# Seven half-size products in place of eight for three input projections, and a transform moved behind them

## The chip, the cores and the metric

One core of one Trainium2 chip runs the whole program. The metric is the device time of one execution in microseconds (us); lower is better.

The engines: TensorE (PE in the profile; its weight loads are PEld), the Vector engine (DVE), the Scalar engine (ACT), GpSimd (POOL), and the Sync engine (SP), which only issues DMAs. All matrix work is float32; the profile records each float32 matmul as two passes, so counts of matmul records are twice those of the code.

## What is computed

One layer of a diffusion backbone on 640 tokens (128 context, 512 latent) of width 1024: modulated norm, a token mixer (an mLSTM part and a Hyena part side by side), norm, and a mixture of 16 experts. The change touches the Hyena part alone:

```python
proj = xm @ p['w_in']                  # xm: 640 tokens x 1024
hy_in = proj[..., ML_QKVO_COLS + ML_GATE_COLS:]       # 3 x 512 columns
u = short_conv(hy_in, p['hy_conv_w'], grid)           # 3 taps along the tokens, per channel
parts = jnp.split(u, HY_ORDER + 1, axis=-1)           # three inputs of 512 channels
z = parts[-1]
for n in range(HY_ORDER):
    z = parts[n] * long_conv(z, filt[n, 0], filt[n, 1], p['hy_bias'][n])   # by FFT
```

## The kernel before

Everything lives in one SBUF tensor (`arena`) and one PSUM tensor of 8 banks (`banks`, 512 float32 columns each). Each engine runs one hand-written program in order; the order of work is set by these programs and by named semaphores. A semaphore counts finished steps (`conv_d` 3 means three short convolutions done).

**Weights** arrive as 21 chunks of 2 MB in a ring of three slots (`chunks`, from line 346), issued by SP at L410 once the chunk three places before has been consumed (`freed`). Chunks 0 to 9, 12 and 14 are pieces of `w_ada` (the modulation), 10, 11 and 13 (`HY_AT`) the three Hyena inputs in the order part 2, part 0, part 1, and 15 to 18 the mLSTM's q, k, v, o.

**Ahead of the Hyena part**, TensorE makes the filters' spectra, then turns the normed input `x_raw` (ten times four transposes, L1716); ACT (L734, L738) and DVE (L1069, L1073) apply the modulation on the way out of PSUM and so write `hT`, the transposed activations, 8 blocks of 128 rows by 640 tokens. Then come `ada_piece(8)` and `ada_piece(9)` (L1622).

**The projections** (`hyena_group(n)`, n = 0 to 11): one group makes 128 channels of one input. `channel_groups` (L1721 to 1727) runs over the 8 row blocks k and multiplies the same 128 x 128 weights with the 512 latent columns (L1725) and the 128 context columns (L1726) of `hT`, into two banks. ACT (`taps`, L752, L753) reads both banks and multiplies by the middle tap; DVE (`short_conv`, L1087 to L1090) adds the outer taps, again from the banks. The first eight results are turned to tokens in rows (`to_tokens`, L1736, L1737) and copied out by ACT (`untranspose`, L759, L760); the last four stay as they are in `part1t`.

**The order**: groups 0 to 8, each followed by the transposes of the one before, with `ada_turn` and `ada_piece` 10 and 11 in between; `ada_turn(2)`; the first forward transform `forward(0)` (L1757, L1759, ten bank fills, copied out by ACT in `spectra`, L778); groups 9 to 11; `project_qk(0)`, four groups of the same form; a transpose of the packed modulation vectors (L1798) and the first inverse transform (L1804, L1808, L1809); `forward(1)`; `project_qk(1)`; and so on.

Beside this, DVE runs after `forward(0)`: `spectrum_of(0)`, `short_conv(9)`, `low_products(0)`, `short_conv(10)`, `high_products(0)`, `short_conv(11)`, `high_sums`, a butterfly (which signals `mul_done` 1), `context_products(0)` (`mul_done` 2), then `ada_columns(1)`, `ada_columns(2)` and four small operations that end in `modB_ready`. TensorE waits for that last signal ahead of L1798:

```python
        project_qk(0)
        pe.wait_ge(S["ld_dft"], 48)
        pe.wait_ge(S["modB_ready"], 1)
        pe.transpose(ps[0:64, 0, 0:P], pack...)          # L1798
        for t in range(NT):                              # first inverse transform
```

Of the kernel before, what the change touches and what calls it, by code (L numbers as in the profile page):

```python
# [13 lines left out]
P = 128  # L14
# [13 lines left out]
ORD = 2  # L28
# [77 lines left out]
def emit(nc, a, stack):  # L106
# [116 lines left out]
    ada_rows = [area(W1 + 6144, CH), area(W4, CH), area(W4 + CH, CH)]  # L223
# [55 lines left out]
    def rt(*shape):  # L279
# [25 lines left out]
    names = """ld_setup ld_mlp ld_w3 ld_hybias ld_dft ld_x ld_late ld_gate ld_state ld_rowctx ld_rowlat  # L305
        ld_x2 ld_route ld_gr2 rows_stored y_zeroed out_stored  all_stored
        ada_done ada_row ada_t mod_ready setup_t cols_ready cvec_ready mlp_done arg_ready hid_ready ones_ready x_rstd xn_ready
        win_ready filt_done filt_read spec_read sq_ready sq_done lanes_read norm_done norm_sqrt norm_stored norm_cols xrs_ready comb_done ab_ready modA_ready modB_ready
        xt_done xt_a xt_d hy_done taps_ready conv_a conv_d tp_done tp_read fw_done fe_read mul_done iv_done iv_read
        packT_ready qk_done qk_read kt_done gate_done gate_read gt_done gt_read row_a row_ready m_ready  # L310
# [3 lines left out]
        lg_done rt_v rt_exp pos_done idx_done tiles_ready route_ready  # L314
# [25 lines left out]
    freed.update({n: ("hy_done", NB * (i + 1)) for i, n in enumerate(HY_AT)})  # L340
# [51 lines left out]
    def _(sp):  # L392
# [70 lines left out]
        sp.wait_ge(S["out_stored"], 64 + 16 * SPILL)  # L463
# [23 lines left out]
    def _(pool):  # L487
# [33 lines left out]
        pool.wait_ge(S["filt_read"], 28)  # L521
        pool.dma_start(area(W6, 1536), a["late"]).then_inc(S["ld_late"], 16)
# [5 lines left out]
                       zeros.unsqueeze(1).broadcast_to((P, KD * KD, P))).then_inc(S["y_zeroed"], 16)  # L528
# [31 lines left out]
        pool.wait_ge(S["out_stored"], 64)  # L560
        pool.wait_ge(S["y_zeroed"], 16)
# [60 lines left out]
    def _(act):  # L622
# [119 lines left out]
        def taps(n):  # L742
            part, blk = ((2, 0, 1)[n // 4], n % 4)
            act.wait_ge(S["hy_done"], n + 1)
            if part != 2:
                act.wait_ge(S["taps_ready"], 2)
            if n >= 2:
                act.wait_ge(S["tp_done"], min(n - 1, 8))
            u = part1t[:, blk, :] if part == 1 else ubuf[:, n % 2, :]
            w = tap(part, blk, 1)  # L750
            b = 1 + 2 * (n % 2)
            link(A(u[:, CTX:TOK], ps[:, b, :], ACT.Copy, scale=w[0]))  # L752
            link(A(u[:, 0:CTX], ps[:, b + 1, 0:CTX], ACT.Copy, scale=w[1]), "conv_a")  # L753

        def untranspose(n):
            blk = n % 4
# [5 lines left out]
        for n in range(9):  # L762
            taps(n)
            if n == 8:
                ada_row(2)
            if n:
                untranspose(n - 1)
# [22 lines left out]
        for n in range(9, 12):  # L790
# [1357 lines left out]
```

## Time and profile before

| | |
|---|---|
| median of 3 runs | 829.66 us (828.74 to 830.28) |
| the profiled execution's own time | 835.36 us |
| its span, first to last instruction | 833.5 us |
| mean granted TensorE clock | 0.985 |
| PE busy | 788.0 us (95% of the span) |
| DVE, ACT, POOL busy | 417.9, 278.2, 111.0 us |
| PE busy on L1725 and L1726 | 164.2 and 61.5 us, 320 records each |
| PE share of the chain that ended last | 84% |

Times in the rows below are from the start of the span. A busy time of a matmul holds its way through the array, which overlaps with the next one; the pace of a stream of matmuls is read from the starts.

### The profile page before, as it was taken

To read this page: it belongs to the slowest core of one execution; us is meant where nothing else is said; L and a number is where in the kernel's file an instruction comes from. 1 tells how busy PE (TensorE), PEld (TensorE's weight loads), DVE (VectorE), ACT (ScalarE), POOL (GpSimd) and SP (SyncE) were. 2 spreads that over 40 slices of the span, in tenths; PEclk is the share of its full clock that TensorE was granted. 3 is DMA by queue.
4 is the path that set the end of the run, shared out by engine and by line. 5 is a ranking of instruction groups with operands and counts; after the bars stand their busy time and mean duration, and the time that the engine had idled before them with its cause. 6 is when DMAs were issued, how large, how long until landed. Compare 5 with 4: busy or idle time off the path is not lost.

```text
span 833.5 us, 16962 instructions
## 1 busy us (share of the span) xinstructions
PE 788.0 (95%) x6753; PEld 457.1 (55%) x6753; DVE 417.9 (50%) x763; ACT 278.2 (33%) x558; POOL 111.0 (13%) x217
## 2 busy tenths in 40 slices
PE   4999899999999999999999999689999999999975
PEld 1232455554555457456775445357777777777741
DVE  3567622223891496664547475833333333333327
ACT  1567802224110211246233243223333333333325
POOL 4000100000001000011002000032222222222221
PEclk9999999999999999989999999889999999999999
DMA  8987450213051802133008574989999999999537
GB/s 257 390 345 298 169 202 3 99 48 155 0 202 57 250 1 102 26 128 114 13 2 314 198 282 150 410 351 423 419 417 416 418 419 420 416 418 416 217 109 289
DMA packets 41973, 195.11 MB, mean 234 GB/s; under 512 B 4873, under 2 KB 5237, under 8 KB 34301
## 3 DMA queue, kind: packets, MB, share of 16 engines
q1 hardware_dynamic: 29944, 156.70, 47.4%
q0 software_dynamic: 9216, 31.10, 10.7%
q10 hardware_dynamic: 2758, 6.52, 2.2%
q8 instruction: 42, 0.69, 0.3%
q14 instruction: 13, 0.11, 0.0%
HBM read 175.75 MB, written 18.55 MB: 233 GB/s over the span
## 4 chain that ended last, share of the span: by engine, by line
PE 84%; DVE 6%; DMA 3%; ACT 3%; issue 3%; POOL 1%; ACTq 0%; DVEq 0%; POOLq 0%
PE banks L2079 20%; PE banks L1725 17%; PE banks L2092 10%; PE banks L1863 4%; PE banks L1726 4%; PE banks L1872 4%; PE banks L1967 3%; PE banks L1670 2%; PE banks L1957 2%; DMA arena<-in_x_sample 2%; PE banks L1622 2%; PE banks L1757 2%; PE banks L1692 1%; PE banks L1925 1%; PE banks L1917 1%
## 5 line engine op out<-in xcount | busy, mean ns | idle before, releaser
L2079 PE MATMUL banks<-arena 128*32 128x256 f32 x3072 | 176.4, 380 | 1.1 <-DVE arena L1548 1.1
L1725 PE MATMUL banks<-arena 128*128 128x512 f32 x320 | 164.2, 595 | 1.5 <-issue 0.8
L2079 PEld LDWEIGHTS banks<-arena 128*32 128x32 f32 x3072 | 120.5, 110 | 48.6 <-issue 2.1
L1726 PEld LDWEIGHTS banks<-arena 128*128 128x128 f32 x320 | 60.8, 190 | 76.5 <-issue 76.5
L2092 PE MATMUL banks<-arena 128*32 128x256 f32 x1536 | 93.0, 379 | 1.2 <-DVE arena L1552 1.2
L1528 DVE STREAM_TRANSPOSE arena<-arena 128x256 f32<-128x256 f32 x49 | 32.1, 655 | 122.5 <-PE banks L2079 113.9
L2092 PEld LDWEIGHTS banks<-arena 128*32 128x32 f32 x1536 | 60.1, 110 | 24.2 <-DVE arena L1552 1.7
L1726 PE MATMUL banks<-arena 128*128 128x128 f32 x320 | 61.5, 274 | 0.0
L928 ACT ACTIVATE arena<-banks 32x256 f32<-32x256 f32 x98 | 36.8, 375 | 71.3 <-PE banks L2092 70.7
L1535 DVE COPY arena<-banks 32x256 f32<-32x256 f32 x98 | 41.4, 422 | 33.0 <-PE banks L2092 32.3
L1725 PEld LDWEIGHTS banks<-arena 128*128 128x128 f32 x320 | 48.6, 192 | 4.8 <-issue 3.3
L590 POOL DMA_INDIRECT arena<-expert_input,arena x47 | 46.4, 987 | 12.4 <-issue 12.4
L1087 DVE SCALAR_TENSOR_TENSOR arena<-banks,arena 128x504 f32<-128x504 f32 x12 | 8.9, 743 | 70.0 <-ACT arena L753 70.0
L752 ACT ACTIVATE arena<-banks,arena 128x512 f32<-128x512 f32 x12 | 8.2, 687 | 97.9 <-PE banks L1726 97.9
L944 ACT ACT_TABLE_LOAD x24 | 30.8, 1283 | 28.7 <-issue 17.1
L947 ACT ACTIVATE arena<-banks 128x128 f32<-128x128 f32 x48 | 13.4, 279 | 79.5 <-PE banks L2079 79.5
L1863 PE MATMUL banks<-arena 128*128 128x512 f32 x80 | 37.6, 632 | 0.0
L1872 PE MATMUL banks<-arena 128*128 128x512 f32 x80 | 36.1, 594 | 0.0
L1967 PE MATMUL banks<-arena 128*128 128x512 f32 x80 | 35.2, 595 | 0.0
L1957 PE MATMUL banks<-arena 128*128 128x512 f32 x80 | 35.2, 593 | 0.0
L587 POOL COPY arena<-arena 128x1 int32 x47 | 8.6, 183 | 163.6 <-DVE arena L1528 163.6
L1863 PEld LDWEIGHTS banks<-arena 128*128 128x128 f32 x80 | 16.1, 204 | 20.1 <-issue 20.1
(388 smaller groups left out, 995.9 us busy)
## 6 DMA issues: line engine op xcount, KB each, us to landing
arena<-in_w_gate SPq DMA_DIRECT2D x15, 2048.0 KB
arena<-in_w_down SPq DMA_DIRECT2D x15, 2048.0 KB
arena<-in_w_up SPq DMA_DIRECT2D x14, 2048.0 KB
arena<-in_w_ada SPq DMA_DIRECT2D x12, 2048.0 KB, 10.1
arena<-in_w_in SPq DMA_DIRECT2D x7, 2048.0 KB, 8.0
expert_output<-arena ACTq DMA_DIRECT2D x49, 128.0 KB
expert_output<-arena POOLq DMA_DIRECT2D x1, 4096.0 KB, 20.4
arena<-in_w_out SPq DMA_DIRECT2D x2, 2048.0 KB, 8.0
```

Source lines behind the costliest of these rows:

```text
L590: pool.indirect_dma_start(xr[n], None, h2_quarters, bass.IndirectOffsetOnAxis(ap=idx_now[n], axis=0))\
L928: ins = act.activation(ysb[n][:, l * 256:(l + 1) * 256], ps[l * LANE:(l + 1) * LANE, 5, 0:256], ACT.Copy)
L1528: dve.transpose(xg, xr[n].rearrange("p (r k) -> p k r", k=KD)).then_inc(S["xg_ready"], 1)
L1535: ins = dve.tensor_copy(ysb[n][:, l * 256:(l + 1) * 256], ps[l * LANE:(l + 1) * LANE, 5, 0:256])
L1725: M(ps[:, b, :], lhs, hT[:, k, CTX:TOK], start=k == 0, stop=k == KD - 1)
L1726: mm = M(ps[:, b + 1, 0:CTX], lhs, hT[:, k, 0:CTX], start=k == 0, stop=k == KD - 1)
L1863: mm = M(ps[:, 1 + n % 4, :], hT[:, k, n * P:(n + 1) * P], w[:, k, :], start=k == 0, stop=k == KD - 1)
L1872: mm = M(ps[:, 1, :], hT[:, k, t * P:(t + 1) * P], w[:, k, :], start=k == 0, stop=k == KD - 1)
L1957: M(ps[:, 1 + 2 * (j % 2) + c, :], part1t[:, k, t * P:(t + 1) * P], w[:, NB + k, :], start=k == 0, stop=False)
L1967: mm = M(ps[:, 1 + 2 * (j % 2) + c, :], ymlT[:, k, t * P:(t + 1) * P], w[:, k, :], start=False, stop=k == NB - 1)
L2079: mm = M(ps[q * LANE:(q + 1) * LANE, 2, 0:2 * P].rearrange("p (g a j) -> p g a j", g=2, j=LANE), xg[:, k, :], gate_up[e % 3][:, :, k, q, : ...
L2092: mm = M(ps[l * LANE:(l + 1) * LANE, 5, 0:256], aT[:, q * LANE:(q + 1) * LANE], w[:, q, l * 256:(l + 1) * 256], start=q == 0, stop=q == FF ...
```

## The change

For each pair of 128-channel blocks the product (1024 rows by 256 channels) x (1024 rows by 640 tokens) is cut in two along the rows, the channels and the tokens. In place of eight half-size products it does seven (Winograd's form of Strassen's scheme), from sums of quarters of the weights (`wsums`) and of the activations (`hs1` to `hs4`), and adds the seven results into two buffers of 640 tokens (`raw`) in SBUF. Each product is 4 matmuls of 128 x 128 weights on 320 columns. DVE makes the sums and all but the first of the additions; ACT copies the first product. `taps` and `short_conv` now read `raw` and not the banks. The blocks are taken in the order 0, 2, 1, 3 of each input.

All twelve blocks (six pairs) now come ahead of `forward(0)`, whose spectral work on DVE and ACT is no longer interleaved with three groups. `ada_piece(8)` moves ahead of the wait for the filters (before the transposes of L1716), `ada_piece(9)` between the first two products. `cosine_halves(1)` and the gate columns move into the pair loop on DVE. The load of `late` on POOL's queue waits for all convolutions rather than for the filters. Some semaphores are merged, and the waits on them count on.

```diff
+    QK, QC, QT = KD // 2, CH // 2, TOK // 2
+    h11, h12, h21, h22 = (hT[:, k * QK:(k + 1) * QK, r * QT:(r + 1) * QT] for r in range(2) for k in range(2))
+    raw = [area(W6 + i * TOK, TOK) for i in range(2)]
+    PAIRS = 6
+    BLOCK_OF = [0, 2, 1, 3] * 3
...
-    freed.update({n: ("hy_done", NB * (i + 1)) for i, n in enumerate(HY_AT)})
+    freed.update({n: ("sw_done", 14 * (i + 1)) for i, n in enumerate(HY_AT)})
...
-        pool.wait_ge(S["filt_read"], 28)
-        pool.dma_start(area(W6, 1536), a["late"]).then_inc(S["ld_late"], 16)
+        pool.wait_ge(S["conv_d"], 2 * PAIRS)
+        pool.dma_start(area(W6, 1536), a["late"]).then_inc(S["ld_route"], 16)
...
+    def product_bank(p, i):
+        return ps[:, 1 + (7 * p + i) % 4, 0:QT]
...
         def taps(n):
-            act.wait_ge(S["hy_done"], n + 1)
+            act.wait_ge(S["sw_d"], 6 * (n // 2) + 5 + n % 2)
...
-            link(A(u[:, CTX:TOK], ps[:, b, :], ACT.Copy, scale=w[0]))
-            link(A(u[:, 0:CTX], ps[:, b + 1, 0:CTX], ACT.Copy, scale=w[1]), "conv_a")
+            link(A(u[:, CTX:TOK], raw[n % 2][:, CTX:TOK], ACT.Copy, scale=w[0]))
+            link(A(u[:, 0:CTX], raw[n % 2][:, 0:CTX], ACT.Copy, scale=w[1]), "conv_a")
...
-        for n in range(9):
-            taps(n)
+        for p in range(PAIRS):
+            act.wait_ge(S["sw_done"], 7 * p + 1)
+            if p:
+                act.wait_ge(S["conv_d"], 2 * p - 1)
+            link(A(raw[0][:, 0:QT], product_bank(p, 0), ACT.Copy), "sw_a")
+            if 1 <= p <= 4:
+                untranspose(2 * p - 2)
+                untranspose(2 * p - 1)
+            if p == 5:
                 ada_row(2)
+            taps(2 * p)
+            taps(2 * p + 1)
...
         spectra(0)
-        for n in range(9, 12):
-            taps(n)
...
+        def early_weight_sums(c):
+            dve.wait_ge(ring_full[HY_AT[c] % 3], 16 * (HY_AT[c] // 3 + 1))
+            w11, w12, w21, w22 = quarters(slot[HY_AT[c] % 3])
+            link(TT(wsums[c][0], w12, w11, ALU.subtract))
+            link(TT(wsums[c][1], w22, wsums[c][0], ALU.subtract))
...
+        early_weight_sums(0)
+        dve.wait_ge(S["xt_a"], 5)
+        link(TT(hs1, h21, h22, ALU.add))
+        link(TT(hs2, hs1, h11, ALU.subtract), "sums_in")
+        third_weight_sum(0)
+        link(TT(hs3, h11, h21, ALU.subtract), "sums_in")
+        fourth_weight_sum(0)
+        link(TT(hs4, h12, hs2, ALU.subtract), "sums_in")
...
+        for p in range(PAIRS):
+            dve.wait_ge(S["sw_done"], 7 * p + 3)
+            dve.wait_ge(S["sw_a"], p + 1)
+            link(TT(right[:, front], left[:, front], product_bank(p, 2), ALU.add), "sw_d")
+            link(TT(left[:, front], left[:, front], product_bank(p, 1), ALU.add), "sw_d")
+            if p == 0:
+                gate_columns()
+            elif p == 1:
+                third_weight_sum(1)
+                fourth_weight_sum(1)
+            elif p == 2:
+                cosine_halves(1)
+            elif p == 3:
+                third_weight_sum(2)
+            dve.wait_ge(S["sw_done"], 7 * p + 4)
+            link(TT(left[:, back], right[:, front], product_bank(p, 3), ALU.add), "sw_d")
+            dve.wait_ge(S["sw_done"], 7 * p + 5)
+            link(TT(right[:, back], left[:, back], product_bank(p, 4), ALU.add))
+            link(TT(right[:, front], right[:, front], product_bank(p, 4), ALU.add), "sw_d")
+            dve.wait_ge(S["sw_done"], 7 * p + 6)
+            link(TT(left[:, back], left[:, back], product_bank(p, 5), ALU.add), "sw_d")
+            short_conv(2 * p)
+            dve.wait_ge(S["sw_done"], 7 * p + 7)
+            link(TT(right[:, front], right[:, front], product_bank(p, 6), ALU.add), "sw_d")
+            short_conv(2 * p + 1)
+            if p == 0:
+                early_weight_sums(1)
+            elif p == 2:
+                dve.wait_ge(S["ada_t"], 2)
+                early_weight_sums(2)
+            elif p == 3:
+                fourth_weight_sum(2)
         spectrum_of(0)
-        short_conv(9)
         low_products(0)
-        short_conv(10)
         high_products(0)
-        short_conv(11)
         high_sums()
...
+        ada_piece(8)
         pe.wait_ge(S["filt_read"], 28)
...
+        def product(p, i, x, w):
+            if 7 * p + i >= 4:
+                q, r = divmod(7 * p + i - 4, 7)
+                if r == 0:
+                    pe.wait_ge(S["sw_a"], q + 1)
+                else:
+                    pe.wait_ge(S["sw_d"], 6 * q + (2, 1, 3, 4, 5, 6)[r - 1])
+            j = p % 2
+            for k in range(QK):
+                mm = M(product_bank(p, i), w[:, k, j * P:(j + 1) * P], x[:, k, :], start=k == 0, stop=k == QK - 1)
+            mm.then_inc(S["sw_done"], 1)
+
+        def hyena_pair(p):
+            c = p // 2
+            w11, w12, w21, w22 = quarters(wait_chunk(HY_AT[c]))
+            t1, t2, t4 = wsums[c]
+            product(p, 0, h11, w11)
+            if p == 0:
+                ada_piece(9)
+            product(p, 1, h12, w21)
+            if 1 <= p <= 4:
+                to_tokens(2 * p - 2)
+            elif p == 5:
+                ada_piece(11)
+            pe.wait_ge(S["sums_in"], (1, 5, 7)[c])
+            product(p, 2, hs2, t2)
+            pe.wait_ge(S["sums_in"], (2, 6, 7)[c])
+            product(p, 3, hs3, w12)
+            if 1 <= p <= 4:
+                to_tokens(2 * p - 1)
+            elif p == 0:
+                ada_turn(1)
+            product(p, 4, hs1, t1)
+            pe.wait_ge(S["sums_in"], (3, 6, 8)[c])
+            product(p, 5, h22, t4)
+            pe.wait_ge(S["sums_in"], (4, 6, 8)[c])
+            product(p, 6, hs4, w22)
...
         def forward(o):
...
                 if o == 0 and g < 4:
-                    pe.wait_ge(S["conv_d"], 8 + g // 2)
+                    pe.wait_ge(S["sw_d"], 6 * PAIRS - 3 + g)
...
-        ada_piece(8)
-        ada_piece(9)
-        for n in range(9):
-            hyena_group(n)
...
+        for p in range(PAIRS):
+            hyena_pair(p)
+            if p == 1:
                 ada_piece(10)
         ada_turn(2)
         forward(0)
-        for n in range(9, 12):
-            pe.wait_ge(S["fe_read"], 10)
-            hyena_group(n)
```

## Rows read from the trace of the kernel before

**Rows 1.** The page: chain that ended last, by engine and by line
```profile
PE 84%; DVE 6%; DMA 3%; ACT 3%; issue 3%; POOL 1%; ACTq 0%; DVEq 0%; POOLq 0%
```

**Rows 2.** Busy by stretch: us, PE, PEld, DVE, ACT, POOL (count), clock, DMA, GB/s
```profile
104.00:205.00 101.00, 100.19 (x420) 54.81 (x420) 24.68 (x45) 22.82 (x45) 0.00 (x0) 1.00 0.28 105
```

**Rows 3.** Timeline of PE, one group: start us, us, line, operands, passes
```profile
164.79 0.64 PE L1736 MATMUL banks<-arena 128*128 128x128 f32 x4
...
165.38 1.02 PE L1725 MATMUL banks<-arena 128*128 128x512 f32 x2
...
166.46 1.02 PE L1725 MATMUL banks<-arena 128*128 128x512 f32 x2
...
174.04 0.64 PE L1736 MATMUL banks<-arena 128*128 128x128 f32 x4
```

**Rows 4.** Timeline of PE around the transposes ahead of the projections
```profile
97.74 1.97 PE L1716 MATMUL banks<-arena 128*128 128x128 f32 x16 [1.09 <-DVE arena L1059]
...
104.36 3.64 PE L1622 MATMUL banks<-arena 128*32 128x512 f32 x32 [1.02 <-ACT arena L738]
```

**Rows 5.** Timeline of DVE: end of the modulation, a 1024-element sum, one short convolution
```profile
101.70 2.56 DVE L1073 TENSOR_SCALAR arena<-banks,arena 128x512 f32<-128x512 f32 x3 [0.17 <-PE banks L1716]
104.30 1.23 DVE L1017 TENSOR_TENSOR arena<-arena 128x1024 f32<-128x1024 f32 x1
...
166.24 0.74 DVE L1087 SCALAR_TENSOR_TENSOR arena<-banks,arena 128x504 f32<-128x504 f32 x1 [6.95 <-ACT arena L753]
...
168.18 0.35 DVE L1090 SCALAR_TENSOR_TENSOR arena<-banks,arena 128x127 f32<-128x127 f32 x1
```

**Rows 6.** Timeline of PE: the first forward transform and the group behind it
```profile
195.81 7.03 PE L1757 MATMUL banks<-arena 128*128 128x512 f32 x16
...
205.30 1.13 PE L1725 MATMUL banks<-arena 128*128 128x512 f32 x2 [0.75 <-ACT arena L778]
```

**Rows 7.** Timeline of DVE from the first spectrum to the modulation vectors
```profile
203.64 2.29 DVE L1096 TENSOR_TENSOR arena<-arena 128x2048 f32<-128x2048 f32 x1 [7.39 <-ACT arena L778]
...
215.51 0.74 DVE L1087 SCALAR_TENSOR_TENSOR arena<-banks,arena 128x504 f32<-128x504 f32 x1 [2.21 <-ACT arena L753]
...
217.83 2.29 DVE L1114 TENSOR_TENSOR arena<-arena 128x2048 f32<-128x2048 f32 x1
...
252.34 0.18 DVE L1183 TENSOR_TENSOR arena<-arena 128x16 f32<-128x16 f32 x1
```

**Rows 8.** Timeline of PE: the transpose behind `project_qk(0)`
```profile
265.98 0.27 PE L1798 MATMUL banks<-arena 128*64 128x128 f32 x1
```

**Rows 9.** Timeline of ACT: the taps of one group, one copy of a spectrum
```profile
165.04 0.69 ACT L752 ACTIVATE arena<-banks,arena 128x512 f32<-128x512 f32 x1 [7.21 <-PE banks L1726]
...
165.76 0.37 ACT L753 ACTIVATE arena<-banks,arena 128x128 f32<-128x128 f32 x1
...
196.92 0.60 ACT L778 ACTIVATE arena<-banks 128x512 f32<-128x512 f32 x1 [0.58 <-PE banks L1757]
```

**Rows 10.** PE by stretch: length us, busy us (records), granted clock, DMA share, GB/s
```profile
370.00:375.00 5.00, 5.00 (x7) 0.50 0.00 0
...
530.00:535.00 5.00, 4.22 (x11) 0.73 0.93 326
```

**Rows 11.** Timeline of PE ahead of and in the first of these stretches
```profile
365.95 1.43 PE L1884 MATMUL banks<-arena 36*128 36x36 f32 x20
...
370.08 9.91 PE L1863 MATMUL banks<-arena 128*128 128x512 f32 x16
```

**Rows 12.** Timeline of PE ahead of and in the second
```profile
527.21 0.64 PE L1989 MATMUL banks<-arena 128*32 128x128 f32 x16 [1.33 <-DVE arena L1412]
...
528.55 4.52 PE L2001 MATMUL banks<-arena 128*128 128x512 f32 x6
```

**Rows 13.** Timeline of POOL: what follows the load of `late` in its queue
```profile
267.74 0.57 POOL L525 DMA_DIRECT2D modulation_rows<-arena  x1 [169.21 <-ACT arena L795]
```

**Rows 14.** The page: DMA issues of `w_in` chunks, KB each, median us to landing
```profile
arena<-in_w_in SPq DMA_DIRECT2D x7, 2048.0 KB, 8.0
```

More of the change, by code:

```diff
@@ L221, in emit, with quarters @@
     shift_sums = gate_taps.rearrange("p a b c d -> p (a b c d)")[:, 0:40].rearrange("p (g n) -> p g n", g=2)
-    ada_rows = [area(W1 + 6144, CH), area(W4, CH), area(W4 + CH, CH)]
+    ada_rows = [area(W1 + 6144, CH), area(W4 + 5120, CH), area(W0 + 5632, CH)]
+    QK, QC, QT = KD // 2, CH // 2, TOK // 2
+    h11, h12, h21, h22 = (hT[:, k * QK:(k + 1) * QK, r * QT:(r + 1) * QT] for r in range(2) for k in range(2))
+    hs1, hs2, hs3, hs4 = (area(W4 + i * QK * QT, QK, QT) for i in range(4))
+    wsums = [tuple(area(x, QK, QC) for x in at3)
+             for at3 in ((W2, W2 + 1024, W0 + 3072), (W2 + 5120, W2 + 6144, W0 + 4608),
+                         (W0 + 3072, W4 + 5120, W0 + 4608))]
+    raw = [area(W6 + i * TOK, TOK) for i in range(2)]
+    PAIRS = 6
+    BLOCK_OF = [0, 2, 1, 3] * 3
+    def quarters(w):
+        return (w[:, k * QK:(k + 1) * QK, c * QC:(c + 1) * QC] for k in range(2) for c in range(2))
     qT = area(W2 + 2560, H, TOK)
@@ L917, in _ @@
         link(A(rt_e, rt_e, ACT.Exp))
-        link(A(rt_d, rt_d, ACT.Exp), "rt_exp")
+        link(A(rt_d, rt_d, ACT.Exp), "wo_rs")
         act.wait_ge(S["tiles_ready"], 2)
@@ L1077, in short_conv @@
         def short_conv(n):
[L1079 removed]
+            part, blk = ((2, 0, 1)[n // 4], BLOCK_OF[n])
             dve.wait_ge(S["conv_a"], n + 1)
             u = part1t[:, blk, :] if part == 1 else ubuf[:, n % 2, :]
[L1082 removed]
             ul = u[:, CTX:TOK].rearrange("p (r x) -> p r x", x=GRID)
[L1084 to L1085 removed]
+            pl = raw[n % 2][:, CTX:TOK].rearrange("p (r x) -> p r x", x=GRID)
+            uc, pc = u[:, 0:CTX], raw[n % 2][:, 0:CTX]
             w0, w2 = tap(part, blk, 0), tap(part, blk, 2)
@@ L1149, in context_products @@
             link(TT(xs, p[2], p[3], ALU.subtract), "mul_done")
-        cosine_halves(1)
-        dve.wait_ge(S["norm_cols"], 32)
-        link(dve.reciprocal(norm_columns, norm_columns))
-        for o in range(ORD):
-            columns = colsT[:, 80:116].rearrange("p (j b) -> p j b", j=3)[:, :, o * NB:(o + 1) * NB]
-            for i in range(2):
-                link(TT(gate_taps[:, o, i], columns, norm_columns[:, o, i, :].unsqueeze(1).broadcast_to((P, 3, NB)), ALU.mult),
-                     "taps_ready" if i else "dve_chain")
@@ L1159, in _, with fourth_weight_sum @@
-        for n in range(9):
-            short_conv(n)
+        def early_weight_sums(c):
[3 more added lines that the diff above has]
+            link(TT(wsums[c][1], w22, wsums[c][0], ALU.subtract))
+        def fourth_weight_sum(c):
+            w11, w12, w21, w22 = quarters(slot[HY_AT[c] % 3])
+            link(TT(wsums[c][2], w21, wsums[c][1], ALU.subtract), "sums_in")
@@ new lines, in third_weight_sum, with gate_columns @@
+        def third_weight_sum(c):
+            w11, w12, w21, w22 = quarters(slot[HY_AT[c] % 3])
+            link(TT(w12, w22, w12, ALU.subtract), "sums_in" if c else "dve_chain")
+        def gate_columns():
+            link(dve.reciprocal(norm_columns, norm_columns))
+            for o in range(ORD):
+                columns = colsT[:, 80:116].rearrange("p (j b) -> p j b", j=3)[:, :, o * NB:(o + 1) * NB]
+                for i in range(2):
+                    link(TT(gate_taps[:, o, i], columns, norm_columns[:, o, i, :].unsqueeze(1).broadcast_to((P, 3, NB)),
+                            ALU.mult), "taps_ready" if i else "dve_chain")
@@ new lines, in _ @@
+        early_weight_sums(0)
[6 more added lines that the diff above has]
+        link(TT(hs4, h12, hs2, ALU.subtract), "sums_in")
+        dve.wait_ge(S["norm_cols"], 32)
+        left, right = raw
+        front, back = slice(0, QT), slice(QT, TOK)
+        for p in range(PAIRS):
[30 more added lines that the diff above has]
+                fourth_weight_sum(2)
@@ L1760, in forward @@
                 mm.then_inc(S["fw_done"], 1)
-        ada_piece(8)
-        ada_piece(9)
-        for n in range(9):
-            hyena_group(n)
-            if n == 8:
-                ada_piece(11)
-            if n:
-                to_tokens(n - 1)
-            if n == 0:
-                ada_turn(1)
-            if n == 3:
+        for p in range(PAIRS):
+            hyena_pair(p)
+            if p == 1:
                 ada_piece(10)
```

58 lines of the change are left out of this document (21 added, 37 removed).

## The prediction

> **What bounds the kernel now.** I read the shares of the chain that ended last first: PE 84% [rows 1]. A change that takes matmul time away pays at full price, as long as no other engine then ends later. Next the busy time by stretch: over the first nine groups PE is busy 100.2 of 101 us at full clock, DVE 24.7 us, ACT 22.8 us [rows 2]. TensorE sets the pace here and the others have three quarters of the time free. Last the timelines, for the pace of a pass and for what each engine waits on. In one group the starts of two k-steps lie 1.08 us apart (165.38, 166.46) and each k-step is two passes of 512 and two of 128 columns [rows 3]: 1.08 / (2 x 640) = 0.844 ns per column and pass. There is no fixed cost beside it: the 16 passes of 512 of the forward transform take 7.03 - 0.16 = 6.87 us, 0.43 us each, which is 0.84 ns per column [rows 6] (0.16 is the last pass's way through the array, as in every such row). Passes of 128 columns go at nearly that rate even when each has weights of its own: the five transposes between 164.79 and 165.38 take 0.12 us each [rows 3]. So a weight load hides behind even a 128-column pass.
>
> **Step 1, the products.** A group is 8 x 1.08 = 8.65 us; twelve are 103.8 us, all on PE. After: 6 pairs x 7 products x 4 k-steps x 2 passes = 336 passes of 320 columns. No pass of 320 stands in the stage before; its bounds are 0.12 us (128 columns) and 0.43 us (512), and since both lie on one line through the rate, I take 320 x 0.844 = 0.270 us. That is 2.16 us a product, 15.1 us a pair, 90.7 us in all. **Gain 13.1 us**, with ends of 103.8 - 336 x 0.12 = 63 us gained and 336 x 0.43 - 103.8 = 41 us lost.
>
> **Step 2, ada_piece(8) moved.** PE is idle 1.09 us ahead of the transposes (waiting for DVE) [rows 4]. The piece takes half of the 3.57 us of two pieces, 1.78 us [rows 4]. The transposes begin at 97.74 [rows 4]; 1.09 us and the last pass's 0.16 before, at 96.5, PE is free. The piece ends at 98.3 and so delays them by 0.6 us; ACT and DVE behind them, which end that phase at 104.26 [rows 5], move by the same 0.6. **Gain 1.2 us.** Its chunk was issued long before, and the chunks freed by it come earlier.
>
> **Step 3, the start of the first pair.** The sums need DVE after its last modulation, now at 104.9 us. A 1024-element sum is 1.23 us plus 0.03 to the next [rows 5]; 2048 elements take 2.29 [rows 7], so 1280 elements take 1.5. Two weight sums and `hs1`, `hs2` are done 5.6 us later, at 110.5; the next two sums at 113.3. PE meanwhile does product 0 (2.2), ada_piece(9) (1.8) and product 1 (2.2), from 105.0 to 111.1, and product 2 to 113.3. The first two waits are hidden, the third by nothing to spare: **loss 0.15 us**. Were ada_piece(9) not in between, it would be 1.9.
>
> **Step 4, the loop of a pair.** An addition of 320 columns out of PSUM is not in the trace; DVE takes 0.35 us for 127 columns and 0.74 for 504, both partly from PSUM [rows 5]. I take 0.55 by the line between them, 0.58 with its gap. DVE then does per pair seven additions (4.1 us), two short convolutions of 2.32 (166.24 to 168.53 and the gap [rows 5]), and beside them nothing to 5.0 us of weight sums and `cosine_halves` (pair 2 has the most): 8.7 to 13.8 us beside PE's 16.3 (15.1 and two `to_tokens` of 0.59). ACT does two taps (1.1 each [rows 9]), a copy and two untransposes, under 5 us. The long way is: product 5, addition, taps on ACT, convolution, addition of product 6, taps, convolution; from the end T of a pair's product 6 it ends at T + 6.4. What the next pair needs from it: `to_tokens` at T + 4.3 needs the first convolution (T + 2.2), the second `to_tokens` (T + 9.2) needs T + 6.4, product 5 (T + 12) needs an addition which DVE makes by T + 10 at the latest. **No loss**; the cover is 2 us where it is thinnest, and each further us of a pair's loop beyond that would cost 6. Additions of 0.74 us (the upper bound) add 1.3 us a pair and still fit; at 0.35 nothing is gained either, since PE sets the pace.
>
> **Step 5, forward(0) behind all.** Its four first banks are free when PE comes (the last addition ends at T + 2.8, PE reaches that bank at T + 3.1). The fifth needs ACT's first copy of 0.60 us [rows 9], and ACT comes free only after the taps of block 11, at T + 3.95: PE waits from T + 3.9 to T + 4.7. **Loss 0.75 us.** The wait of 0.75 us behind the transform was there before [rows 6] and stays.
>
> **Step 6, the cover that goes.** Before, DVE's work from the first spectrum (203.64) to the last of the modulation vectors (252.52) lay beside seven groups, and PE came to L1798 at 265.98 [rows 7, 8], 13.5 us later. Now it lies beside four. DVE's chain without the three convolutions (2.32 each) and the idle 2.2 us [rows 7] is 48.9 - 7.0 - 2.2 = 39.7 us. PE starts `project_qk(0)` 1.66 us after the chain's start (205.30 - 203.64), does four groups of 8.67 us ((265.98 - 205.30) / 7) and comes to L1798 at 36.3 us. `modB_ready` is last in DVE's order, behind the context products, so it becomes what L1798 waits for: 39.9 - 36.3, **loss 3.6 us**. `mul_done` 1, at 34, would have been in time: it is the modulation vectors that are late, not the spectrum. Behind L1798 in PE's queue stands the inverse transform, and behind it everything.
>
> **Step 7, the clock.** An idle stretch of this length is nowhere in PE's warm time. What stretches with little work do: after 4 us of 36- and 5-column matmuls the granted clock is 0.50, which is 1.2 GHz, and 16 passes take 9.91 us in place of 7.03 [rows 10, 11], 2.9 us lost. In the routing, after idle gaps of which the longest is 1.33 us, 6 passes take 4.52 us in place of 2.74, 1.8 lost [rows 10, 12]. With 1.09 and 1.02 us idle in 8 us [rows 4] it stays at 2.4 GHz. 3.6 us without any work is nearly three times the longest gap of the routing stretch, so I expect the fall, at **2.2 us** between 1.8 and 2.9 (0 if it doesn't come).
>
> **Step 8, the rest.** `late` goes out some 115 us later; POOL's queue behind it waits for `packT_ready` until 267.74 [rows 13], so nothing is held, and its readers come after 300 us. SP's weight chunks are freed in the same order. The tightest is the third input's: freed when pair 1 ends, first read by DVE behind pair 2's convolutions some 20 us later, and such a chunk lands 8.0 us after its issue [rows 14]. Merged semaphores cost nothing. All that follows the inverse transform is released by what is ahead of it and moves as a block.
>
> **Sum.** -13.1 - 1.2 + 0.15 + 0.75 + 3.6 + 2.2 = -7.6 us. The profiled execution took 835.36 us (span 833.5) and the median of the runs is 829.66; the 5.7 us between them I leave on both sides. 829.7 - 7.6 = **822.1 us**.
>
> **The rivals.** (a) The stall comes and the clock stays at 2.4 GHz: 819.9. For it: the longest single gap that rows 12 have is 1.33 us, in a stretch of small matmuls. Against it: that stretch was enough, and this gap is longer. (b) DVE is in time at L1798, from a faster chain: 829.7 - 13.4 = 816.3. Against it: every term of the 39.7 us is from rows. (c) The hand-offs of step 4 have less cover than I count: PE waits 0.3 to 1.0 us in each pair, 2 to 6 us in all, 824 to 828. For it: the loop crosses three engines six times, and 0.1 us at each crossing is 0.6 us of a pair. (d) On the other side: TensorE falls to 1.2 GHz within the products. The engine now waits on a semaphore ahead of each of 42 products; a pass at the lower clock costs 0.27 us more, so from 7.6 / 0.27 = 28 of the 336 passes on the kernel is slower than before. With a third of them it is 852. Against it: forward(0), which waits for a bank at every fill, runs at 0.43 us a pass [rows 6]. (e) A 320-column pass costs as much as one of 512: 41 us lost where 13.1 are gained, 876. Against it: both widths on one line.
>
> The Trainium skill bears on (d): "TensorE: Matmul & The Clock Gate", in "A second HAM failure mode: psum-queue depth-cycling", says that a kernel which cycles through PSUM banks between matmul groups can leave TensorE briefly idle so often that its clock swings between the levels. By it the time would be that of (d); the forward transform, which cycles through the same four banks at full clock, does not agree. The same page, in "HAM oscillation", holds that long idle gaps between bursts bring the lower clock back, which is the case of step 7; rows 11 and 12 agree.
>
> **How the numbers follow.** Forecast 0.50; (a) 0.20; (b) 0.08; (c) 0.15; (d) 0.05; (e) 0.02. A change under 0.2% (1.7 us) can't be told from none in this kernel. A third of (c)'s upper part falls within that, so faster 0.90, same 0.03, slower 0.07. The range takes in (a), the forecast with the bounds of steps 5 to 7, and most of (c): 817.5 to 826.5; (b), (d), (e) and the end of (c) are left out.
>
> **What would show it.** Starts of product passes 0.27 us apart, 15.1 us a pair; PE busy without gaps from 105 to 207 us (step 4); one gap of 0.7 us in the forward transform; a gap of 3.6 us ahead of the transpose of L1798, released by DVE's last modulation product; the first 16 passes of the inverse transform in 9 us or so in place of 7.03, with granted clock 0.50. The forecast is wrong if gaps recur in every pair, if the product passes are not on the line of the rate, or if the gap at L1798 is missing.

## The result and the profile after

The changed kernel takes **820.95 us** (median of 4 runs, 820.21 to 822.52) against 829.97 us for the kernel before on the same chip: ratio 0.9889, 95% interval 0.9867 to 0.9912. The forecast was 822.1. A later set of 5 runs gave 821.07; where a run below is set against the changed kernel, 821.0 stands for both. The sets were timed on several chips, on which the kernel before took 829.4 to 830.0 us, so a difference of medians below about 1 us says little by itself.

The profiled execution took 820.9 us, which is the median to 0.1 us, with a span of 819.1 us. That is 14.4 us less than the span of before, more than the 9.0 of the medians. The difference lies where the kernels do the same: the four passes ahead of the transposes' wait (L1688 before, L1763 after) start at 94.77 us before, 2.97 us ahead of the first row of [rows 4], and at 90.03 after, so 4.7 of the 5.7 us by which the profiled execution of before was above its median were lost at its start. Between that point and the small transpose behind `project_qk(0)` (L1798 before, L1894 after) there are 171.2 us before and 161.1 after, **10.1 us less**; from there to the end 567.5 and 568.0. The first of these two stretches is called the **stage** below. Its length is read from one trace of each kernel. It leaves out the start and the end of the program, in each of which the traces of this case differ by several us.

The page of after: busy time by engine, and the chain that ended last.

```profile
PE 771.0 (94%) x6705; PEld 487.7 (60%) x6705; DVE 459.1 (56%) x821; ACT 281.0 (34%) x564; POOL 110.6 (14%) x217
...
PE 78%; DVE 10%; DMA 4%; issue 3%; ACT 3%; POOL 1%; ACTq 0%; POOLq 0%; DVEq 0%
```

DVE has 41 us more work than before and its share of the chain has gone from 6 to 10%: a part of what TensorE lost in work is now waited for. The six pairs, by engine (columns as in [rows 2]):

```profile
100.00:203.00 103.00, 102.69 (x434) 70.68 (x435) 67.05 (x107) 22.58 (x45) 0.00 (x0) 1.00 0.23 86
```

TensorE is as full as in [rows 2] and at full clock; DVE has gone from 24.7 to 67 us. Timeline of PE in after: `ada_piece(8)`, the transposes and the first pair.

```profile
91.84 1.93 PE L1697 MATMUL banks<-arena 128*32 128x512 f32 x16
...
100.31 2.39 PE L1825 MATMUL banks<-arena 128*128 128x320 f32 x8 [1.02 <-ACT arena L755]
102.64 1.93 PE L1697 MATMUL banks<-arena 128*32 128x512 f32 x16
104.49 6.73 PE L1825 MATMUL banks<-arena 128*128 128x320 f32 x24
111.06 0.60 PE L1711 MATMUL banks<-arena 128*128 128x128 f32 x4
111.49 10.93 PE L1825 MATMUL banks<-arena 128*128 128x320 f32 x40
```

The 40 passes of the last row take (10.93 - 0.16) / 40 = 0.269 us each, where [rows 3, 6] gave 0.844 ns a column. The idle 1.09 us of [rows 4] ahead of the transposes is gone. The waits of 0.8 and 1.0 us for ACT behind it were there before too. From 100.31 to 202.50 us no gap of PE is listed. Then the forward transform and the small transpose, which answer to [rows 6, 8]:

```profile
202.50 3.60 PE L1866 MATMUL banks<-arena 128*128 128x512 f32 x8
206.75 3.70 PE L1866 MATMUL banks<-arena 128*128 128x512 f32 x8 [0.65 <-ACT arena L800]
...
213.00 1.10 PE L1801 MATMUL banks<-arena 128*128 128x512 f32 x2 [0.84 <-ACT arena L800]
...
247.47 0.38 PE L1802 MATMUL banks<-arena 128*128 128x128 f32 x2
251.10 0.27 PE L1894 MATMUL banks<-arena 128*64 128x128 f32 x1 [3.25 <-DVE arena L1258]
251.21 7.03 PE L1900 MATMUL banks<-arena 128*128 128x512 f32 x16
```

and DVE there, which answers to [rows 7]:

```profile
211.25 2.29 DVE L1115 TENSOR_TENSOR arena<-arena 128x2048 f32<-128x2048 f32 x1 [2.78 <-ACT arena L800]
...
248.98 0.69 DVE L1168 TENSOR_TENSOR arena<-arena 128x512 f32<-128x512 f32 x1
249.71 0.41 DVE L1024 TENSOR_TENSOR arena<-banks,arena 128x32 f32<-128x32 f32 x2
...
250.78 0.18 DVE L1258 TENSOR_TENSOR arena<-arena 128x16 f32<-128x16 f32 x1
```

The gap of 3.25 us ends when L1258, the last of the modulation vectors, does; the chain from 211.25 to 250.96 is 39.7 us long. In this execution the 16 passes behind the gap run at full clock (7.03 us, as in before).

The number in brackets is not the whole of what a wait costs. It counts from the end of the last pass's way through the array (0.16 us), and a stream that was broken starts a few hundredths slower. So costs are read from the starts. Without a wait the small transpose starts 0.22 us behind the row ahead of it, as in before, where [rows 8] has it at 265.98:

```profile
265.76 0.39 PE L1726 MATMUL banks<-arena 128*128 128x128 f32 x2
```

In after it starts 3.63 us behind (247.47 to 251.10): the wait costs 3.4 us. The one in the forward transform costs 0.8 us: 8 passes of 0.43 us would bring TensorE from 202.50 to 205.94, and it starts at 206.75.

### The profile page after: what moved, and what is told of

The parts are those of the page before. It is cut to its first block, busy times and chain, and to the rows that moved or that the text cites. A ratio compares the mean times of both kernels' runs of the same rounds, so it can differ in the third digit from the quotient of the medians.

```text
span 819.1 us, 16982 instructions
## 1 busy us (share of the span) xinstructions
PE 771.0 (94%) x6705; PEld 487.7 (60%) x6705; DVE 459.1 (56%) x821; ACT 281.0 (34%) x564; POOL 110.6 (14%) x217
## 4 chain that ended last, share of the span: by engine, by line
PE 78%; DVE 10%; DMA 4%; issue 3%; ACT 3%; POOL 1%; ACTq 0%; POOLq 0%; DVEq 0%
PE banks L2175 20%; PE banks L1825 11%; PE banks L2188 9%; PE banks L1959 4%; PE banks L1968 4%; PE banks L1801 3%; PE banks L2063 3%; PE banks L2053 3%; DMA arena<-in_x_sample 2%; PE banks L1697 2%; PE banks L1767 2%; PE banks L1745 2%; PE banks L1866 1%; PE banks L2021 1%; PE banks L2029 1%
## 5 line engine op out<-in xcount | busy, mean ns | idle before, releaser
L2175 PE MATMUL banks<-arena 128*32 128x256 f32 x3072 | 188.3, 382 | 1.2 <-DVE arena L1623 1.1
L2175 PEld LDWEIGHTS banks<-arena 128*32 128x32 f32 x3072 | 138.6, 111 | 28.5 <-issue 3.7
L2188 PE MATMUL banks<-arena 128*32 128x256 f32 x1536 | 103.6, 379 | 1.4 <-DVE arena L1627 1.2
L1825 PE MATMUL banks<-arena 128*128 128x320 f32 x336 | 93.0, 434 | 1.0 <-ACT arena L755 1.0
L2188 PEld LDWEIGHTS banks<-arena 128*32 128x32 f32 x1536 | 72.7, 110 | 19.4 <-DVE arena L1627 1.7
L1825 PEld LDWEIGHTS banks<-arena 128*128 128x128 f32 x336 | 62.8, 190 | 28.3 <-issue 2.5
L1801 PE MATMUL banks<-arena 128*128 128x512 f32 x128 | 65.7, 595 | 1.7 <-ACT arena L800 1.7
L1802 PEld LDWEIGHTS banks<-arena 128*128 128x128 f32 x128 | 24.3, 190 | 30.6 <-issue 30.6
L1959 PE MATMUL banks<-arena 128*128 128x512 f32 x80 | 36.6, 618 | 0.0
L1968 PE MATMUL banks<-arena 128*128 128x512 f32 x80 | 36.1, 594 | 0.0
L2063 PE MATMUL banks<-arena 128*128 128x512 f32 x80 | 35.2, 595 | 0.0
L2053 PE MATMUL banks<-arena 128*128 128x512 f32 x80 | 35.2, 592 | 0.0
L768 ACT ACTIVATE arena<-arena 128x512 f32<-128x512 f32 x12 | 8.7, 722 | 56.1 <-DVE arena L1227 38.1
L1959 PEld LDWEIGHTS banks<-arena 128*128 128x128 f32 x80 | 15.6, 197 | 19.5 <-issue 19.5
L808 ACT ACTIVATE arena<-banks 128x512 f32<-128x512 f32 x8 | 4.8, 597 | 64.7 <-PE banks L1802 64.7
```

Source lines behind the costliest of these rows:

```text
L1801: M(ps[:, b, :], lhs, hT[:, k, CTX:TOK], start=k == 0, stop=k == KD - 1)
L1825: mm = M(product_bank(p, i), w[:, k, j * P:(j + 1) * P], x[:, k, :], start=k == 0, stop=k == QK - 1)
L1959: mm = M(ps[:, 1 + n % 4, :], hT[:, k, n * P:(n + 1) * P], w[:, k, :], start=k == 0, stop=k == KD - 1)
L1968: mm = M(ps[:, 1, :], hT[:, k, t * P:(t + 1) * P], w[:, k, :], start=k == 0, stop=k == KD - 1)
L2053: M(ps[:, 1 + 2 * (j % 2) + c, :], part1t[:, k, t * P:(t + 1) * P], w[:, NB + k, :], start=k == 0, stop=False)
L2063: mm = M(ps[:, 1 + 2 * (j % 2) + c, :], ymlT[:, k, t * P:(t + 1) * P], w[:, k, :], start=False, stop=k == NB - 1)
```

## The experiments

My theory: seven products save their eighth share in full, because TensorE paces the pair loop; what is given back is given back at one place, the small transpose, since DVE's chain lost its cover. The rivals were a loss in every pair, a spectral chain that is too long as such, and a clock that does or doesn't fall behind the gap. Times are medians; each ratio is to the kernel before on the same chip, with its 95% interval. The ratios are those on record and not quotients of the two medians, from which they differ by up to 0.0015.

### Is it the modulation vectors that are late?

```diff
+        ada_columns(1) ... modB_ready        # the block of six operations
         spectrum_of(0)
...
         context_products(0)
-        ada_columns(1) ... modB_ready
```

> The changed kernel with the two ada_columns and the four operations behind them moved ahead of spectrum_of(0), into DVE's idle 2.8 us. Theory A (the modulation vectors, last in DVE's order, are what TensorE waits for): the gap of 3.25 us ahead of the small transpose is gone, mul_done 1 comes some 2 us before TensorE needs it, no new gap; 3.2 us faster than the changed kernel, about 817.7. Theory B (DVE's spectral chain as a whole is too long for four groups): the gap moves from the transpose to the first inverse matmul and stays above 2 us; time as the changed kernel within 1 us, about 820.5.

Measured (e1): 816.83 us, ratio 0.9851 (0.9836 to 0.9866), 4.2 us less than the changed kernel. The stage takes 157.7 us in place of 161.1, 3.4 less, which is the whole cost of the wait. Its timeline of PE around the small transpose:

```profile
247.75 0.27 PE L1894 MATMUL banks<-arena 128*64 128x128 f32 x1
247.86 7.03 PE L1900 MATMUL banks<-arena 128*128 128x512 f32 x16
```

and its timeline of DVE, from the last modulation vector to the product that sets `mul_done` 1:

```profile
209.63 0.17 DVE L1251 TENSOR_TENSOR arena<-arena 128x16 f32<-128x16 f32 x1
211.31 2.29 DVE L1115 TENSOR_TENSOR arena<-arena 128x2048 f32<-128x2048 f32 x1 [1.50 <-ACT arena L800]
...
243.08 2.29 DVE L1116 SCALAR_TENSOR_TENSOR arena<-arena 128x2048 f32<-128x2048 f32 x1
```

The gap is gone and didn't move: the six operations lie in DVE's former idle time, and `mul_done` 1 (the end of the last row, 245.4) is 2.4 us ahead of L1894. Theory A holds. That the medians gain 4.2 us and the stage 3.4 is taken up below, under the clock.

### The order alone, with eight products

The kernel before with its twelve groups ahead of `forward(0)`:

```diff
-        for n in range(9):
+        for n in range(12):
             hyena_group(n)
...
-        for n in range(9, 12):
-            pe.wait_ge(S["fe_read"], 10)
-            hyena_group(n)
```

> The kernel before with only the order changed: all twelve groups (eight products each) ahead of forward(0). Theory A (lost cover): a gap of 3.3 to 3.6 us ahead of the small transpose, as in the changed kernel, since DVE's chain of 39.7 us lies beside the same four groups; and one of 3 us at the first bank of forward(0), which here must wait for the last convolution (it reads the banks). Together 6 to 7 us slower than the kernel before, about 836. Theory B (the gap comes from the products, through DVE's additions): no gap ahead of the transpose, at most 3 us slower, about 833.

Measured (e3): 839.0 us (834.94 to 844.56), ratio 1.012 (1.0088 to 1.0151). PE at the forward transform and at the small transpose:

```profile
220.23 8.54 PE L1752 MATMUL banks<-arena 128*128 128x512 f32 x16 [3.18 <-DVE arena L1088]
...
269.42 0.27 PE L1790 MATMUL banks<-arena 128*64 128x128 f32 x1 [3.29 <-DVE arena L1178]
269.53 7.03 PE L1796 MATMUL banks<-arena 128*128 128x512 f32 x16
```

The same 3.3 us gap ahead of the transpose stands in a kernel without a single addition of products: it belongs to the order. At the first bank there is the other gap, 3.18 us, and behind that one the clock fell (8.54 in place of 7.03 us). Gaps and clock sum to some 8 us, and the stage is 8.1 us longer than before (179.3 against 171.2); the median lies 9.1 above before, over the 6 to 7 expected, in which the clock was left out. The changed kernel does not have this gap at the first bank: its convolutions read SBUF, so the bank is free once the products have been added.

### What a product is worth, and how much DVE may cost

> The changed kernel with product 6 of each pair computed twice (the second time overwrites the first), so eight products a pair. Theory A (products cost their columns and lie on the path): 6 x 2.16 = 13 us more than the changed kernel, about 834, a little more than the kernel before: the whole gain of the seven products is given back. Rival (part of a product hides behind the additions of DVE): under 9 us more.

Measured (e10): 833.21 us, ratio 1.0036 (1.0013 to 1.0058), 12.2 us more than the changed kernel. The rows are from its timeline of PE. Where after has 40 passes between two transposes, this one has 48; the last row is the forward transform:

```profile
150.27 13.09 PE L1826 MATMUL banks<-arena 128*128 128x320 f32 x48
...
215.38 7.03 PE L1867 MATMUL banks<-arena 128*128 128x512 f32 x16
```

13.09 - 10.93 = 2.16 us a pair, to the hundredth what step 1 gave a product; in the pair loop no part of it hides, and six make 13.0 us. The stage is only 12.0 us longer (173.1 against 161.1), and the medians say 12.2. The difference is in the last row: its 16 passes have no wait between them. While the last product is made a second time, DVE and ACT finish the block ahead of it, so ACT's last taps end 2.0 us behind the last product (216.94 against 214.94 us) where they end 4.0 behind it in after (206.07 against 202.07), and the wait of step 5 is gone.

The next two put one and two operations of 2.3 us behind each of the first five pairs on DVE:

```diff
             short_conv(2 * p + 1)
+            if p < PAIRS - 1:
+                dve.wait_ge(S["spec_read"], 12)   # long met by then
+                for _ in range(1):      # 2 in the second kernel
+                    link(TT(h, h, h, ALU.max))   # h = spec_h[:, 0, 0, 0:4, :]
```

> The changed kernel with one more DVE operation of 2048 elements (2.3 us, a maximum of an array with itself, which changes nothing) behind each of the first five pairs. Step 4 put the thinnest cover at 2 us, behind pairs 0 and 2, which have further weight sums there: gaps of about 0.4 us at product 5 of pairs 1 and 3, none elsewhere; 0.5 to 1 us slower than the changed kernel, about 821.6. Rival (hand-offs have less cover than counted, the case c of the prediction): gaps in every pair, 3 us or more.

Measured (e6): 822.4 us, ratio 0.9902 (0.9871 to 0.9933), 1.4 more than the changed kernel; the stage is 1.2 us longer (162.3). Its two gaps of PE in the pair loop, and no others:

```profile
129.93 4.54 PE L1830 MATMUL banks<-arena 128*128 128x320 f32 x16 [0.38 <-DVE arena L1211]
...
165.03 8.85 PE L1830 MATMUL banks<-arena 128*128 128x320 f32 x32 [0.34 <-DVE arena L1211]
```

They are in pairs 1 and 3 ahead of product 5, waiting for the addition that frees its bank, as step 4 had it. By the starts they cost 0.5 us each, so the cover there was 1.8 us.

> As e6 with two such operations, 4.65 us a pair. DVE then has 13.4 to 18.5 us of work a pair beside 16.3 of TensorE. Step 4: gaps of 2.5 to 3 us behind pairs 0 and 2 and of 0.2 to 1 us behind the others, 6 to 8 us slower than the changed kernel, about 828. Rival (DVE paces only by its sum of work, the order of the waits does not matter): only pair 2's 2.2 us, 823.

Measured (e7): 830.5 us, ratio 1.0008 (0.9985 to 1.0031): the whole gain is gone. All gaps of PE in its pair loop:

```profile
132.65 4.54 PE L1830 MATMUL banks<-arena 128*128 128x320 f32 x16 [2.71 <-DVE arena L1211]
...
171.36 10.54 PE L1830 MATMUL banks<-arena 128*128 128x320 f32 x32 [3.95 <-DVE arena L1211]
...
190.40 8.85 PE L1830 MATMUL banks<-arena 128*128 128x320 f32 x32 [0.88 <-DVE arena L1211]
```

The brackets sum to 7.5 us, by the starts the gaps cost 8.1, and behind the longest one there is a clock loss of 1.7 (32 passes in 10.54 in place of 8.85 us): 9.8 us, against 10.0 in the stage (171.1) and 9.5 by the medians. The order of the waits counts, not the sum of the work. The gap behind pair 2 is 1 us longer than I gave it, and behind pairs 1 and 4, where I expected small ones, there is none.

### The ends of the pair loop

`ada_piece(9)` after pair 0 and not between its first products:

> The changed kernel with ada_piece(9) after pair 0 and not between its products 0 and 1, so the sums of DVE have 1.8 us less cover. Step 3: products 2 and 3 of pair 0 wait 1.3 and 0.5 us for their sums (the changed kernel waits under 0.1 there), 1.8 us slower than the changed kernel, about 822.7. Rival (the sums are ready earlier than counted): no gap, time as the changed kernel.

Measured (e9): 822.28 us, ratio 0.9903 (0.9872 to 0.9933), 1.3 more than the changed kernel. PE at the start of pair 0's products:

```profile
106.07 2.42 PE L1825 MATMUL banks<-arena 128*128 128x320 f32 x8 [0.98 <-DVE arena L1199]
108.85 2.42 PE L1825 MATMUL banks<-arena 128*128 128x320 f32 x8 [0.36 <-DVE arena L1201]
```

Both waits are where they were expected. The brackets sum to 1.34 us; by the starts the waits cost 1.2 and 0.6 us, the 1.8 that were expected, and the stage is 1.9 us longer (163.0). The 1.3 of the medians is within their scatter.

`ada_piece(8)` alone moved, in the kernel before:

> The kernel before with only ada_piece(8) moved ahead of the wait for the filters. Step 2 gave 1.2 us: of its 1.78 us, 1.1 fill an idle stretch and the rest delays the transposes by 0.6. Expected 828.7 against 829.9. Rival: the delay of the transposes moves ACT and DVE by the whole 1.78, gain 0, 829.9.

Measured (e2): 827.79 us over 12 runs (825.33 to 833.98), ratio 0.9989 (0.997 to 1.0009), unclear by the times. The trace gives it: from the start of the four passes ahead of the wait to the first group 13.16 us before (94.77 to 107.93), 12.15 here (89.08 to 101.23). So 1.0 us, as in the whole stage (170.2 against 171.2); a time of this size is read from a trace, not from medians.

### The clock behind the gap

Two kernels lengthen the gap by one and two operations of 2.33 us on DVE ahead of the modulation vectors:

```diff
+        for _ in range(1):              # 2 in the second kernel
+            link(TT(prod, prod, prod, ALU.max))
         ada_columns(1)
```

> The changed kernel with one more DVE operation of 2048 elements (2.33 us, changes nothing) ahead of the modulation vectors, so TensorE is idle 5.6 us there and not 3.25. Step 7 expected the clock to fall to 1.2 GHz behind such a gap. Theory A (a gap of 3.25 us was too short, one of 5.6 is not): granted clock 0.50 behind it, the 16 passes behind it take over 8.5 us in place of 7.03; 2.3 us of gap and 1.7 to 3 us of clock, 825 to 826. Theory B (a gap does not bring the clock down here): 7.03 us, 823.3.

Measured (e4): 823.05 us, ratio 0.9932 (0.9908 to 0.9955).

> As e4 with two such operations: idle 7.9 us. Theory A: the clock falls for certain, 4.65 us of gap and 1.7 to 3 us of clock, 827.3 to 828.6; DVE's next chain is not on the path. Theory B: 825.6.

Measured (e5): 825.98 us, ratio 0.9962 (0.9939 to 0.9986). The timeline of PE in the first:

```profile
253.00 0.39 PE L1896 MATMUL banks<-arena 128*64 128x128 f32 x1 [5.58 <-DVE arena L1260]
253.18 8.36 PE L1902 MATMUL banks<-arena 128*128 128x512 f32 x16
```

and in the second:

```profile
255.02 0.40 PE L1896 MATMUL banks<-arena 128*64 128x128 f32 x1 [7.92 <-DVE arena L1260]
255.21 8.58 PE L1902 MATMUL banks<-arena 128*128 128x512 f32 x16
```

The clock falls, and the 16 passes take 1.33 and 1.55 us more than 7.03 (mean granted clock 0.74 and 0.65 from 250 to 255 us). But the times rise by 2.1 and 5.0 us over the changed kernel, about the gaps' own 2.33 and 4.65, where theory A had 1.7 to 3 us on top. By the times that is nearer to theory B, by the traces it is theory A; the intervals of the ratios, 1.9 us to each side, rule out neither. Both fit if most executions of the changed kernel already pay for the clock, and its first trace was the exception. Two more runs asked that: the changed kernel again, and one with three matmuls in the gap:

```diff
         project_qk(0)
+        for _ in range(3):
+            M(ps[:, 6, :], ident, area(W0, CH), start=True, stop=True)
         pe.wait_ge(S["modB_ready"], 1)
```

> The changed kernel as it is, a second trace and more times, on one chip with e11. Theory A: its trace may show the fall behind the gap (16 passes in 8.5 to 8.7 us in place of 7.03), which the first one did not, and its times spread over 1.5 to 2 us. Theory B: 7.03 us again.

Measured (e12): 821.07 us (820.69 to 824.04), ratio 0.9894 (0.9874 to 0.9914). In its trace the clock fell (granted 0.50 from 253 to 256 us):

```profile
253.60 0.39 PE L1894 MATMUL banks<-arena 128*64 128x128 f32 x1 [3.25 <-DVE arena L1258]
253.79 8.32 PE L1900 MATMUL banks<-arena 128*128 128x512 f32 x16
```

This execution took 824.04 us, 3.1 more than the profiled one of after. Of that the fall is 1.4; 2.5 us were lost ahead of the stage, whose start is at 92.52 and not 90.03 us. What follows the 16 passes took 0.7 us less. So a single execution's time does not tell whether the clock fell.

> The changed kernel with three matmuls on 512 columns (six passes, 2.6 us, their result is read by nobody) at the start of the gap ahead of the small transpose, so TensorE is idle under 1 us there. The gap's end is set by DVE and stays. Theory A (the clock falls behind the bare gap in most executions, at 1.5 to 1.7 us each): the granted clock stays at 2.4 GHz there in every execution, 0.8 to 1.2 us faster at the median than the changed kernel. Theory B (the fall behind the gap is rare): time as the changed kernel within 0.4 us.

Measured (e11): 820.18 us (818.94 to 824.48), ratio 0.989 (0.9866 to 0.9914). Its timeline of PE:

```profile
246.79 2.74 PE L1894 MATMUL banks<-arena 128*128 128x512 f32 x6
250.11 0.30 PE L1896 MATMUL banks<-arena 128*64 128x128 f32 x1 [0.58 <-DVE arena L1258]
250.25 7.03 PE L1902 MATMUL banks<-arena 128*128 128x512 f32 x16
```

The clock stays up and the median is 0.8 to 0.9 us lower, but the two intervals are nearly the same: the times alone do not show a gain. What follows rests on the traces. Over all traces with this gap between 3.25 and 3.29 us, the 16 passes behind it took 7.03 us in two (the first of after, e3) and 8.54, 8.73, 8.73, 8.73, 8.32 in five (e6, e7, e9, e10, e12). In e6 and e12 the small transpose itself already took 0.39 us in place of 0.27, so the clock fell within the gap; in e7, e9 and e10 it took 0.27 and the clock fell behind it. So the fall is frequent and not certain, and costs 1.3 to 1.7 us. The five cost 7.9 us together, over the seven traces 1.1 us each, an estimate from few traces; with the 3.4 us of the wait it also accounts for e1's 4.2 within the scatter of the medians.

### A kernel faster than both

e1, and the first group of `project_qk` waits only for the copies that have read its two banks:

```diff
-            pe.wait_ge(S["fe_read"], 10 + 10 * which)
+            pe.wait_ge(S["fe_read"], 8 + 10 * which)
             for n in range(NB):
+                if n == 1:
+                    pe.wait_ge(S["fe_read"], 10 + 10 * which)
```

> The kernel of e1, and the first group of each project_qk waits only for the spectra copies that have read its two banks (8 of 10), the second group for all 10. Both waits of 0.84 us behind the two forward transforms should go: 1.5 us faster than e1, about 816.2. Against: the saved 0.8 us is taken from the cover of the first inverse transform, which has some 2 us, so it should hold; if it doesn't, only 0.8 us of it stays.

Measured (e8): **814.48 us** (812.93 to 814.81), ratio 0.9818 (0.9805 to 0.9832). PE at the small transpose, and the 16 passes that answer to the last of [rows 11]:

```profile
246.38 0.27 PE L1896 MATMUL banks<-arena 128*64 128x128 f32 x1
246.48 7.43 PE L1902 MATMUL banks<-arena 128*128 128x512 f32 x16
...
349.30 7.13 PE L1961 MATMUL banks<-arena 128*128 128x512 f32 x16
```

Both waits of 0.84 us are gone, and the 16 inverse passes take 7.43 in place of 7.03 us: 0.4 us is lost again to DVE, which reads the first inverse bank only when its spectral chain is done. From the start of the stage to the first group of `project_qk(1)` there are 177.1 us in e1 and 175.5 here: 1.7 us less, where 1.5 were expected. The median fell by 2.35.

In the profiled execution the clock also stayed up in the stretch of 5-column matmuls where it falls in before [rows 11]. The other traces say how often that is. The same 16 passes took 7.13 us in two of the 14 traces (e8, e9), 8.83 in nine (among them after, e12 and e2) and 9.54 to 10.13 in three (before, e1, e11). So the 7.13 us are most likely luck of this execution and not a gain of e8, and the 9.91 of [rows 11] is one of the three dear cases; the usual fall costs 1.7 us there too.

## Why the prediction was right or wrong

**What bounds the kernel**: right. TensorE paced these products before and after, and a product taken away or added counted in full in the pair loop (13.0 us for six added); of the six added, 0.8 us came back at the forward transform, so that stage and medians show 12.0 and 12.2.

**Step 1**: 13.1 forecast; 0.269 us a pass make 90.4 us, 13.4 saved. The line between 128 and 512 columns held, and rival (e) is out. **Step 2**: 1.2 forecast, 1.0 measured in e2's trace. **Step 3**: 0.15 forecast, about 0.1 measured; e9 shows the waits where they were put, at the size they were given. **Step 4**: no loss, right. The additions take 0.49 us, not 0.55, and the cover of 2 us is 1.8 by e6; rival (c) is out. **Step 5**: 0.75 forecast, 0.8 measured (0.65 in the bracket), and e10 shows that it goes when ACT has time. **Step 6**, the one cost of any size: 3.6 forecast, 3.4 measured (3.25 in the bracket), and e1 and e3 show its cause from two sides. Of the 0.2 us, 0.1 is that TensorE starts its four groups 1.75 us behind the start of DVE's chain and not 1.66. Rival (b), no stall, is what e1 makes: 816.8 us, where it was put at 816.3. **Step 8**: from the small transpose to the end 568.0 against 567.5 us; as the other twelve traces have 564.7 to 568.6 there, a cost below some 2 us can't be told from none. Without the clock the steps gave -9.8 us to the small transpose. The measured terms sum to -13.4 - 1.0 + 0.1 + 0.8 + 3.4 = -10.1, and that is what the stage has.

**Step 7** is the term that was mis-sized. The mechanism is real, but I took it as certain and priced it at 2.2 us, between the 1.8 and 2.9 of [rows 11, 12]. The 2.9 was one of three dear cases in 14 traces; the usual price in that stretch is 1.7. Behind a single bare gap with full work after it, it costs 1.3 to 1.7 us whether the gap is 3.3, 5.6 or 7.9 us long, and behind the 3.3 it came in five traces of seven. The sign named for it, 9 us or so for the 16 passes, is missing in the first trace (7.03) and was 8.3 to 8.7 in the five. Its mean is near 1.1 us, and with that the sum is 829.97 - 10.1 + 1.1 = 821.0, where 820.95 was measured. That it meets the median so closely is luck, since start and end of the program move by more than a microsecond from trace to trace. By the time alone nothing would be decided: the median lies midway between the forecast (822.1) and rival (a), a stall without the fall (819.9), and the changed kernel mixes the two. The rows called in agreement with the sentence of the Trainium skill on long idle gaps ("TensorE: Matmul & The Clock Gate", "HAM oscillation") hold no idle gap over 1.33 us and so did not bear on it; e4 and e5, with gaps of 5.6 and 7.9 us, do agree with it.

**Rival (d)**, the clock falling within the products: 42 waits for a free bank or a sum, of which none held TensorE by more than 0.1 us, and granted clock 1.00 throughout. What the prediction cited for it from the Trainium skill ("TensorE: Matmul & The Clock Gate", "A second HAM failure mode: psum-queue depth-cycling") needs brief idle times between the groups, and there were none, so this case does not test it. e7, which made a long one (3.95 us), lost 1.7 us of clock behind it.

**Left open**: what decides whether the clock falls behind the same gap. Two traces of one unchanged kernel differ.

## What to carry to other kernels

A faster form of one engine's work also shortens the cover it gave to the others: take the longest chain of the other engines that ends in a wait of this one, and count again what lies beside it. Here the last link of that chain was 1.3 us of small operations which needed nothing from it; moving them cost nothing and gained 3.4 us, a quarter of what the seven products had. In a loop across three engines, count the latest time at which each result is needed, not each engine's sum of work: e7's DVE was some 2 us over in one pair only, and its gaps cost 8.1. And read what a wait costs from the starts of two rows, not from the bracket: 3.4 and not 3.25, 0.8 and not 0.65.

## What was not expected of the hardware

The cost of a fall of TensorE's clock behind a gap does not grow with the gap: 1.5 us behind 3.18 us, 1.3 to 1.7 behind 3.25 to 3.27, 1.7 behind 3.95, 1.33 behind 5.58, 1.55 behind 7.92. And it is not sure: 7.03 us for the same 16 passes behind 3.25 and 3.29 us idle in two traces of seven. Behind the gap of 2.71 us in e7 it stayed up. The stretch of 5-column matmuls, the same in all kernels here, is no surer: no loss in two of 14 traces, 1.7 us in nine, 2.4 to 3.0 in three.
